# A macaron transformer block on eight cores: weight loads released by TensorE's progress, gate weights cast in DRAM, a new order in the branch stage

## The reference

```python
h = h + 0.5 * swiglu(rms_norm(h, ffn1_norm), ffn1_w_in, ffn1_w_out)     # width 2816
u = rms_norm(h, mix_norm)
qa, ka, va, qb, kb, vb, f_logit, g_a, g_b = split(u @ w_in)
log_f = log_sigmoid(f_logit + b_forget)
y_a = sliding_window_sink_attention(qa, ka, va, attn_sinks) @ w_branch_a  # 8 heads, 2 kv heads
y_b = forgetting_attention(qb, kb, vb, log_f) @ w_branch_b                # 8 heads, causal
h = h + (sigmoid(g_a) * y_a + sigmoid(g_b) * y_b) @ w_out
h = h + 0.5 * swiglu(rms_norm(h, ffn2_norm), ffn2_w_in, ffn2_w_out)
return rms_norm(h, final_norm)                                            # meta tokens dropped
```

## Time and profile before

| | us |
|---|---|
| runs shown (three) | 3078.96, 3082.65 (the median), 3473.34 |
| profiled execution | 3091.04 |
| its span on the slowest core (7) | 3089.5 |
| spans of the other cores | 3053.6 to 3078.2 |
| TensorE busy on core 7 | 2916.4 (94% of the span) |
| VectorE, ScalarE, POOL busy | 1212.2, 924.7, 548.7 |

### The profile page before, as it was taken

One profiled execution on the slowest core, in us unless ns is written; L12 is line 12 of the kernel. 1 busy time (PEld: TensorE's weight loads), 2 busy tenths in 40 slices (PEclk: granted clock), 3 DMA queues, 4 the chain that ended last, 5 costly groups with the idle time before them and its releaser, 6 DMA issues.

```text
span 3089.5 us, 48484 instructions; the slowest of 8 cores (3053.6 to 3089.5 us)
## 1 busy us (share of the span) xinstructions
PE 2916.4 (94%) x16740; PEld 1317.8 (43%) x16740; DVE 1212.2 (39%) x2075; ACT 924.7 (30%) x1673; POOL 548.7 (18%) x1140
## 2 busy tenths in 40 slices
PE   4999999899998989999989999999999998999997
PEld 2444444344443434444434444444444343444443
DVE  3323234555442333333454323455553243333335
ACT  2101112158882221111231111124888322111112
POOL 6000002200112430000262000130011244000004
PEclk9789999999999999999999999999999999999998
DMA  9121322500127592123395121360011759121102
GB/s 212 32 34 18 52 45 86 119 8 8 36 44 148 101 170 35 18 35 51 90 202 102 28 35 29 84 154 8 7 37 33 149 107 152 29 45 35 18 8 103
DMA packets 143822, 209.06 MB, mean 68 GB/s; under 512 B 91600, under 2 KB 91856, under 8 KB 143072
## 3 DMA queue, kind: packets, MB, share of 16 engines
q0 software_dynamic: 36576, 108.05, 21.7%
q1 hardware_dynamic: 105280, 93.41, 11.4%
q10 hardware_dynamic: 1728, 4.49, 0.6%
HBM read 259.42 MB, written 33.55 MB: 95 GB/s over the span
## 4 chain that ended last, share of the span: by engine, by line
PE 82%; DMA 8%; issue 3%; DVE 3%; POOL 2%; ACT 1%; DVEq 0%; SPq 0%; POOLq 0%; ACTq 0%
PE ps L651 74%; PE ps L1031 3%; DMA uT<-amem 3%; PE ps L1055 3%; DMA amem<-wg 2%; DMA hmem<-x 2%; DMA amem<-w1i 1%; POOL rs L539 1%; POOL nt L539 1%; PE ps L1092 1%; PE ps L1120 1%; ACT amem L988 1%; DVE amem L1004 1%; DVE amem L579 0%; PE ps L1012 0%
## 5 line engine op out<-in xcount | busy, mean ns | idle before, releaser
L651 PE MATMUL ps<-uT,amem 128*128 128x512 bf16 x7488 | 1714.4, 386 | 69.1 <-DVE amem L710 28.2
L651 PEld LDWEIGHTS ps<-uT,amem 128*128 128x128 bf16 x7488 | 723.5, 99 | 946.4 <-issue 183.4
L651 PE MATMUL ps<-amem 128*128 128x512 bf16 x3584 | 805.8, 381 | 9.8 <-DVE hmem L725 8.8
L704 ACT ACTIVATE amem<-ps 128x512 f32<-128x512 f32 (+1 forms) x374 | 214.1, 572 | 1475.7 <-PE ps L651 1453.9
L710 DVE TENSOR_TENSOR amem<-amem,ps 128x512 bf16<-128x512 f32 x352 | 241.8, 687 | 900.5 <-PE ps L651 885.9
L651 PEld LDWEIGHTS ps<-amem 128*128 128x128 bf16 x3584 | 336.9, 98 | 454.6 <-issue 98.3
L725 DVE SCALAR_TENSOR_TENSOR hmem<-ps,hmem 128x512 f32<-128x512 f32 x512 | 353.3, 691 | 248.2 <-PE ps L651 245.7
L988 ACT ACTIVATE amem<-ps,hmem 128x512 bf16<-128x512 f32 (+3 forms) x640 | 352.2, 629 | 44.6 <-PE ps L1055 26.5
L569 ACT ACTIVATE uT<-hmem 128x1024 bf16<-128x1024 f32 x128 | 134.9, 1054 | 237.0 <-DVE hmem L1213 104.4
L1192 DVE SCALAR_TENSOR_TENSOR amem<-amem,ps 128x512 f32<-128x512 f32 x128 | 87.3, 686 | 230.7 <-PE ps L651 230.6
L579 DVE SCALAR_TENSOR_TENSOR amem<-hmem,rs,gb 128x1024 bf16<-128x1024 f32 x96 | 122.3, 1280 | 112.3 <-DMA uT<-amem 53.9
(11 more groups left out here) (110 smaller groups left out, 1179.6 us busy)
## 6 DMA issues: line engine op xcount, KB each, us to landing
amem<-wg POOLq DMA_DIRECT2D x32, 768.0 KB, 7.5
amem<-w1i POOLq DMA_DIRECT2D x44, 512.0 KB, 7.3
amem<-w2i POOLq DMA_DIRECT2D x44, 512.0 KB, 10.5
hmem<-x SPq DMA_DIRECT2D x32, 512.0 KB, 10.5
hsp<-hmem SPq DMA_DIRECT2D x32, 512.0 KB, 2.9
hmem<-hsp SPq DMA_DIRECT2D x32, 512.0 KB, 9.9
out<-hmem SPq DMA_DIRECT2D x32, 512.0 KB, 3.2
amem<-w1o POOLq DMA_DIRECT2D x44, 256.0 KB, 9.2
```

Of the source, the lines that this page charges most:

```text
L651: ins = e.matmul(outv(bk[0]), lhsT=l, rhs=r, start=(i0 + i == 0), stop=(i0 + i == tot - 1))
L704: on("act", lambda e: e.activation(out=tmps[j].ap[:, 0:n], in_=ps[:, bk[0], 0:n], func=AF.Silu), n, [S.bk(bk[0])], [tmps[j].k()])
```

## The change

- **Start.** `clear_meta` comes first; the gain is loaded on ScalarE's queue right after cb; the constants move to SP's queue behind x (`load_consts`), the exp of the sinks into the first projection. Gates order x and the first pass's weights. The second pass's weights are loaded during the first.
- **Norms.** `rsqrt` of norms with `by_pe` (the first FFN1 and its meta tokens) runs on VectorE. `utb` has three buffers.
- **Loads.** `add` takes `after`, an operation to wait for. `ffn1_plan` and `ffn2_plan` give each weight load of the next pass a step (a chunk of a tile) of the current one, behind whose last matmul POOL issues it.
- **Casts.** `wg` and `ww` are cast once, by twelve DRAM to DRAM copies in passes 1 and 2 of the first FFN1, to `wgs` and `wws`, from which both sequences load bf16.
- **Branch stage.** A third wg buffer after attention, eleven blocks of h reloaded at once, the first FFN2 weights one by one, eight PSUM banks for phase 1, for `proj(0)` and `wout`, four (4 to 7) for the FFN's output part.

```diff
@@ Prog.add
+        if after is not None:
+            op.deps.add(after)
+        if eng == "pe":
+            self.last_pe = op.idx
...
+    wgs_d = nc.dram_tensor("wgs", [8, 128, 24 * 128], BF16, kind="Internal").ap()
+    wws_d = nc.dram_tensor("wws", [8, 128, D], BF16, kind="Internal").ap()
...
-        dma("act", t[:], src, [], [t.k()], f"c{i}", 0.2)
-    on("act", lambda e: e.activation(out=esink[:], in_=esink[:], func=AF.Exp), 8, [esink.k()], [esink.k()])
+            dma("sp", t[:], src, [], [t.k()], f"c{i}", 0.2)
...
-    utb = [A_(90112 + 2048 * i, [128, D], f"ut{i}") for i in range(4)]
+    utb = [A_(96256 - 2048 * i, [128, D], f"ut{i}") for i in range(3)]
...
-                on(RS_ENG, fn, 1, rd, wr, cost=0.3)
+                on(eng, fn, 1, rd, wr, cost=0.3 if eng == "pool" else 0.17)
...
-            rsqrt(nr, col, then)
+            rsqrt(nr, col, then, "dve" if on_dve else RS_ENG)
...
-                                [4, 5], done, f"wo{gp}.{b}", split=8))
+                                [4, 5, 6, 7], done, f"wo{gp}.{b}", split=8))
...
+            loads = plan(p)
+            for t in [0] + (["m"] if meta else []) + [1, 2, 3]:
                 for ch in range(nch):
                     call_w_in(w_in, gp, t, ch)
-                if t == 3:
-                    call(lambda gp=gp: hooks("wi", gp))
+                    if t != "m":
+                        for fn in loads.pop(nch * t + ch, ()):
+                            call(lambda fn=fn: fn(P.last_pe))
...
+            return ALL_BANKS if t == 0 else F_BANKS
...
+        WG_OFF = [0, 6144, 86016]
...
-            dma("pool", t.ap.rearrange("p k n -> p (k n)"), wg_d[m], [], [t.k()], f"wg{m % 2}", 1.5)
+            dma("pool", t.ap.rearrange("p k n -> p (k n)"), wgs_d[m], [("wgs", m)], [t.k()], f"wg{slot}", 0.75)
...
             def attention_over():
+                load_wg(2, 1, 2)
                 load_ww()
-                for b in range(8):
+                for b in range(11):
                     reload_h(b)
...
+            both(0)
+            call(lambda: load_wg(3, 1, 0))
+            both(1)
+            call(lambda: load_wg(4, 1, 1))
+            both(2)
+            call(lambda: load_wg(5, 1, 2))
             for b in range(8):
-                call(lambda b=b: _expand(lambda: wout(b, banks2)))
+                call(lambda b=b: _expand(lambda: wout(b, ALL_BANKS)))
+            both(3)
+            call(lambda: load_wg(6, 1, 0))
+            both(4)
+            call(lambda: hooks("chunk", 3))
+            both(5)
+            call(lambda: load_wg(7, 1, 2))
+            for ch in (4, 5, 2):
+                call(lambda ch=ch: hooks("chunk", ch))
+            both(6)
+            for ch in (0, 1):
+                call(lambda ch=ch: hooks("chunk", ch))
+            both(7)
+            call(lambda: [reload_h(b) for b in range(11, 16)])
...
-            call(lambda: hooks("end"))
...
+    load_wi(0, 0, 0, gate=[h[1].k()])
+    load_wi(0, 0, 1)
+    load_wi(0, 0, 2)
+    for b in range(4, 8):
+        load_x(0, b, [wi_t[0, 1].k()])
+    load_wi(0, 0, 3, gate=[h[5].k()])
+    load_wi(0, 0, 4)
+    load_wi(0, 0, 5, gate=[h[7].k()])
+    for b in range(8, 12):
+        load_x(0, b, [wi_t[0, 4].k()])
+    for ch in range(6):
+        load_wo(0, 0, ch, gate=[h[11].k()])
+    for b in range(12, 16):
+        load_x(0, b, [wo_t[0, 3].k()])
+    load_consts()
...
+    def cast_wg(m):
+        return lambda after: dma("pool", wgs_d[m], wg_d[m], [], [("wgs", m)], f"cg{m % 2}", 1.5, after)
+
+    def cast_ww(k):
+        return lambda after: dma("pool", wws_d[k:k + 2], ww_d[k:k + 2], [], [("wws", k), ("wws", k + 1)], f"cw{k % 4}", 1.0, after)
...
+            if p == 3:
+                first, qa = mix[s]["early"]
+                return spread([lambda after: load_gain(1)] + first + qa, [0, 0, 1, 2, 3, 4, 5, 6, 7, 8, 9, 10, 16, 17, 18, 19])
+            wi, wo = weights(0, gp + 1)
+            if p == 0:
+                return spread(wi + wo, list(range(6, 18, 2)) + list(range(18, 24)))
...
+            casts = [cast_wg(m) for m in range(8)] + [cast_ww(k) for k in range(0, 8, 2)]
+            mine = casts[:6] if p == 1 else casts[6:]
...
+                          list(range(0, 10, 2)) + list(range(10, 15)) + list(range(9, 20, 2))[:6])
...
+            wi, wo = weights(1, gp + 1)
+            n = len(wi)
+            if p == 0:
+                return spread(wi + wo, list(range(6, 6 + 2 * n, 2)) + list(range(6 + 2 * n, 6 + 3 * n)))
```

More of the change, by code:

```diff
@@ L136, in ready, with add @@
         return t
-    def add(self, eng, fn, reads=(), writes=(), dma=None, full=False, attach=False, cost=0.0, hold=0.0):
+    def add(self, eng, fn, reads=(), writes=(), dma=None, full=False, attach=False, cost=0.0, hold=0.0, after=None):
         reads, writes = list(reads), list(writes)
@@ L475, in nxt, with dma @@
         return rot[name]
-    def dma(eng, out, in_, reads, writes, slot, mb):
-        P.add(eng, lambda e: e.dma_start(out=out, in_=in_), reads=reads, writes=writes, dma=slot, cost=mb / 0.25)
+    def dma(eng, out, in_, reads, writes, slot, mb, after=None):
+        P.add(eng, lambda e: e.dma_start(out=out, in_=in_), reads=reads, writes=writes, dma=slot, cost=mb / 0.25, after=after)
     def dma_t(out, in_, reads, writes, slot, cost):
@@ L678, in load_wi, with load_wo @@
         wi_t[gp, ch] = t
-        dma("pool", t.ap.rearrange("p a k n -> p (a k n)"), wi_d[f][m], [], [t.k()], f"wi{q}_{ch}", 1.0)
-    def load_wo(f, gp, ch):
+        dma("pool", t.ap.rearrange("p a k n -> p (a k n)"), wi_d[f][m], list(gate), [t.k()], f"wi{q}_{ch}", 1.0, after)
+    def load_wo(f, gp, ch, after=None, gate=()):
         q = gp % 2
@@ L685, in load_wo, with ffn @@
         wo_t[gp, ch] = t
-        dma("pool", t[:], wo_d[f][m], [], [t.k()], f"wo{q}_{ch}", 0.5)
-    def ffn(f, s, meta, tail, hooks):
+        dma("pool", t[:], wo_d[f][m], list(gate), [t.k()], f"wo{q}_{ch}", 0.5, after)
+    def ffn(f, s, meta, tail, plan):
         gp0 = 8 * s + 4 * f
@@ L761, in ffn @@
                 pend.append(mk_out(gp, t))
+            assert not loads
         flush()
@@ L959, in proj @@
             if t == 0:
-                Dq.append(Call(lambda: n_ut.__setitem__(0, 4), gate=lambda: open_norms[0] == 0 and not S.q["t"]))
+                Dq.append(Call(lambda: n_ut.__setitem__(0, 3), gate=lambda: open_norms[0] == 0 and not S.q["t"]))
             call(lambda: fgate_acts(1 + 4 * t, 4, 128))
             if first:
+                call(sink_exp)
                 call(lambda: fgate_acts(0, 1, 48))
@@ L1257, in queue, with both @@
-            call(lambda: [reload_h(b) for b in range(8, 16)])
-            call(lambda: [hooks("chunk", ch) for ch in range(3)])
+            def both(m):
+                call(lambda: _expand(lambda: [branch(m, t, wg_t[m, 1], ALL_BANKS) for t in (2, 3)]))
+            both(0)
[4 more added lines that the diff above has]
+            call(lambda: load_wg(5, 1, 2))
+            for b in range(8):
+                call(lambda b=b: _expand(lambda: wout(b, ALL_BANKS)))
```

207 lines of the change are left out of this document (85 added, 122 removed).

## The result

The changed kernel takes 2965.74 us (median of 4 runs, 2963.2 to 2967.42); the kernel before took 3081.1 us beside it. The ratio is 0.9626, with a 95% interval of 0.9607 to 0.9644: 115 us, or 3.7%, faster. The forecast was 2960. Some executions of most kernels here run some per cent longer, at a lower clock on one die; all times are medians of the others, of which u_two has only two and u_tail one, so that these two have no interval.

The account below looks back on a forecast made before the run. TensorE bound the kernel, losing time to waits and slow clock. Terms 33 + 30 + 31 + 4 + 10 + 3 = 111 us off core 7's 3089.5 gave 2959 (without its 0.81 clock) or 2980; it took 2960, range 2920 to 3030.

Parts of the forecast that it names:

- Start: Start to unbroken TensorE: reordered, gated loads cut the loss from 57 to 24 us, gaining 33 (20 to 40).
- Newton steps on VectorE: First FFN1's norms: moving the steps from POOL costs some 1 us a block in a load-paced stage, so nothing.
- Casts: Twelve wg and ww casts to DRAM in passes 1 and 2: 52 us of casting queue, hidden, so nothing.
- the rival that POOL jams on them: Casts run one after another, output weights queue behind them on POOL, TensorE stands 250 us: 3210 us; chance 0.05.
- Branch stage: Waits for gate weights: bf16 loads, third buffer and new order bring back 30 of 34 us (low end 20).
- FFN2: FFN2's start: second-pass weights released one by one free the transposes; 31 of 35 us on core 7, 47 on core 1.
- FFN1 of sequence 1: Start of this stage: 4 of the 7 us lost come back (0 to 7), since POOL's Newton chains remain.
- the rival that the norms and not the loads hold FFN2's and FFN1's start: POOL's Newton chains keep VectorE waiting even with free transposes; 3015 us, or 3000 without core 7's slow clock; chance 0.13.
- Projection: Waits for PSUM copies: eight banks for tile 0 gain 7 us, half that for the second sequence, 10 (4 to 15).
- FFN output on four banks: Output part of the FFN: four PSUM banks gain 3 us (0 to 5).
- The released loads' waits: Loads issued by POOL wait on TensorE with later Newton steps queued behind: nothing, at most a step of 3.4 us.
- Throttle: Rival: a denser TensorE drops to clock 0.81 through FFN stages; 3060 us for one, 3160 from two; chance 0.04.

Follow-up runs that it names:

- u_two: Changed kernel with two gate-weight (wg) buffers after attention in place of three, still bf16: 2963.5 and 2971.4 us in two runs.
- u_tail: Changed kernel with the old end of the mixer: old h reloads, first-pass FFN2 weights behind them, second-pass weights in one burst: 3025.1 us, single run.
- u_start: Changed kernel with the old start: load order, sinks' exp, Newton steps on POOL, second pass's weights in one go: 2990.5 us.
- x_meta: Changed kernel in which the meta tokens' norm takes a bf16 buffer only for its scaling: 2963.0 to 2963.6 us, ratio 0.9624.
- x_fin: Changed kernel with x_meta's edit, the meta tokens' norm moved behind block 5, and x_late's later loads: 2948.4 us.
- u_newton: Changed kernel with only the Newton steps of the first FFN1's norms back on POOL, new loads and gates kept: 3008 us.
- u_f32: Changed kernel without the DRAM copies: wg and ww loaded from float32, three wg buffers and new order kept: 2979.5 us.
- u_burst: Changed kernel with the second FFN2 pass's weights issued in one burst at the end of the mixer, as before: 2984.5 us.
- x_late: Changed kernel with second-pass loads of sequence 1's FFN1 released from the third tile on (steps 14 to 23, not 6 to 23): 2952 us.
- x_dve: Changed kernel with the Newton steps of sequence 1's x norms on VectorE in place of POOL: 2967.1 us.
- u_banks: Changed kernel with the first projection back on two PSUM banks (6 and 7): 2983.7 us.
- after: The changed kernel itself, from which all follow-up kernels start: 2965.74 us against 3081.1 for the kernel before.

## Why the prediction was right, and where it was not

The sum was 127 us on core 1; its trace gave 117. Its terms, in the order of the prediction:

- **Start, 33: mis-sized, some 25 measured** (u_start; 27 between the two traces of core 1), inside its bounds of 20 to 40. The step that failed is that the stage is paced by loads, so that TensorE has its first matmul at 10 to 13 us and has done 80 by 44. Transposes began at 14, but FFN matmuls at 28 to 34, and core 1 had done 50 by 44; yet its second weight chunk had landed at 20.4 (chain of waits), and no wait for a weight follows. What holds the first tile, as the timelines show it, is the order of work on VectorE and ScalarE: Newton chains, the meta tokens' norm and statistics of later blocks ahead of the scalings and the copy it needs. Where a part of this was mended (x_meta, x_fin), the first matmul came 4 to 5 us earlier, and in x_fin about half of that was lost again around the meta tokens; this was in no term. The other parts were not tried.
- **Newton steps on VectorE, nothing: wrong in the reason, and the size was not tried by itself.** The steps take 0.15 to 0.27 us and a block's chain some 1.9 us with its gaps, not 1, and the chains stand ahead of the first tile's scalings. But the prediction costed the move as a matter of speed. It is what makes the gates possible: on POOL these chains stand behind the gated issues until 56.7 us, which costs 42 us (u_newton). The prediction listed five gates and did not ask what else is queued on POOL behind them.
- **Casts, nothing: right** (u_f32). They landed in 8.5 and 5.6 us, and the rival that POOL jams on them did not come about. For the ww casts (two matrices each), the Trainium skill's rule on how many engines a DMA is spread over (DMA: Bandwidth & Descriptors, "Why a DMA increments its semaphore by 16 and not by 1") had given an estimate of 26 us each; 5.6 us was measured, so the rule as the prediction applied it does not hold for this copy.
- **Branch stage, 30 of 34: right in size**, 32 on core 1 and 34 on core 7; the wait for wg has at most 2.5 us in one piece on core 1 (2 were allowed). The working gave bf16 and the third buffer a part each. The runs show that either alone does most of it and that the buffer adds nothing to bf16.
- **FFN2, 31 on core 7 and 47 on core 1: right in kind, 42 and 44 measured** (over the whole stages, where the 35 to be won on core 7 were two windows). The mechanism, transposes that wait beside weight loads, is shown by u_burst and u_tail. But the prediction put all of it on the second pass's loads; these are about 19, and the earlier reload of h and the first pass's weights are 30 or more (u_tail, one run).
- **FFN1 of sequence 1, 4 of 7: the sign is wrong**, 3 to 8 us worse. The step that failed is the same reading, not carried over: "POOL's Newton chains remain". The change releases the same kind of loads from the second tile on while the last transposes of the new x still run beside loads of x. They cost 14 us there (x_late), and moving the chains beside them wins nothing (x_dve). So the rival that the norms and not the loads hold FFN2's and FFN1's start (0.13) did not come about.
- **Projection, 10: too small, 15 to 18** (u_banks). The prediction gave 7 us to the first sequence and half of that to the second; put back, the two banks cost 4.5 and some 8 us in the two projections, and 0.5 to 2 more in each attention, which was not counted.
- **FFN output on four banks, 3:** not tried by itself, and open.
- **The released loads' waits, nothing:** POOL stands 1292 us for line 663 in after, but no load that it issues stands on TensorE's list of waits except those of wg (3.2 us), and x_dve, which takes norms off POOL, gains nothing.
- **Throttle:** the clock did not fall under a denser TensorE; the mean of the profiled execution is 0.989 to 0.994 on all cores, and the 0.81 of the kernel before did not come again in it. There it held longer, and not on core 7 alone: cores 6 and 7 had 0.81 in 55 to 75 us too, and both in 100 to 220.

The terms that were too large (start 8, FFN1 7 to 12) and those that were too small (projection 5 to 8, FFN2 on core 7 11) nearly cancel, and that is luck: the mechanisms were right in the main, but 2960 was nearer than its terms. Of the two sums, 2959 and 2980, the one without core 7's clock applied. Put back one at a time, the start (25), the end of the mixer (59, one run), the gate weights (26) and the banks (18) cost 128 us together; less the 3 to 8 us that FFN1 of sequence 1 lost, that is close to the 115 that the change won, so no large part of it is left unexplained.

## What to carry to other kernels

A transfer that a stage waits for, here a transpose of 3 us, is worth protecting from bulk loads. Look at every place where loads are released whether such transfers still run, and release them behind the last one: the same edit gave 19 us in FFN2 and left a wait of 14 in FFN1, and shifting the first of its loads there by eight steps took that away. Before a gate is put on an engine's queue, list what else that queue holds. And of two remedies for one wait try each alone: here the second added nothing to the first.

## What the runs showed of the hardware

- A DMA transpose of a block lands in 3.1 to 3.3 us in the median of long stretches, and beside 512 KB weight loads in 12.4 (before, FFN2's start) to 17.5 us (u_burst); in the worst case here (u_tail) one took 39.8.
- A load of 0.79 MB of bf16 from DRAM lands in 5.2 us; the cast from float32 of the same weights into DRAM took 8.5 (after, medians).
- The six Newton steps take 1.9 us on VectorE (after) and 3.35 us on POOL (u_newton) with what lies between them; on POOL some chains are shorter, 2.5 us, when their integer step takes 0.19 us in place of 1.00.
- Around the small matmuls of the meta tokens the granted clock fell to half, 1.2 GHz, and stayed there 6.8 us in after and 10.2 us in x_fin, on all eight cores.
